# A two-block transformer kernel on one core: the first weight slab of each stage in two pieces, two slabs' low halves on VectorE, token transposes at an earlier place

## The reference, cut to what matters

```python
# first block, twice (l = 0, 1)
h = rmsnorm(x, pre_g[l])
u_a, v_a, g_a, q, k, v, g_b = split(h @ w_in[l])            # 1024 -> 2816
y_a = u_a * (spatial_w @ layernorm(v_a) + spatial_b) * silu(g_a)
y_b = attention(rope(rmsnorm(q)), rope(rmsnorm(k)), v) * silu(g_b)
x = x + rmsnorm(concat(y_a, y_b) @ w_out[l], post_g[l])
# second block, once
h = concat(pad, meta_tokens, x)
sb_q, sb_k, sb_v, sw_q, sw_k, sw_v, sb_z, sw_z, g_sb, g_sw = split(rms_norm(h) @ w_in_2)
o_sb = stick_breaking_attention(sb_q, sb_k, sb_v)
o_sw = sliding_window_sink_attention(rope(sw_q), rope(sw_k), sw_v, sinks)
y = sigmoid(g_sb) * ((o_sb * silu(sb_z)) @ w_branch_sb) + sigmoid(g_sw) * ((o_sw * silu(sw_z)) @ w_branch_swa)
out = rms_norm(h + y @ w_out_2)[:, 128:]
```

## Time and profile before

| | us |
|---|---|
| median of 3 runs | 1041.55 (1040.52 to 1042.21) |
| the profiled execution | 1039.15 |
| its span, first to last instruction | 1037.4 |
| TensorE busy | 992.3 (96%) |
| VectorE busy | 631.5 (61%) |
| ScalarE busy | 478.0 (46%) |
| GpSimd busy | 249.3 (24%) |

### The profile page before, as it was taken

One profiled execution on the slowest core, in us unless ns is written; L12 is line 12 of the kernel. 1 busy time (PEld: TensorE's weight loads), 2 busy tenths in 40 slices (PEclk: granted clock), 3 DMA queues, 4 the chain that ended last, 5 costly groups with the idle time before them and its releaser, 6 DMA issues.

```text
span 1037.4 us, 13824 instructions
## 1 busy us (share of the span) xinstructions
PE 992.3 (96%) x5063; PEld 833.5 (80%) x5063; DVE 631.5 (61%) x937; ACT 478.0 (46%) x841; POOL 249.3 (24%) x168
## 2 busy tenths in 40 slices
PE   5999999999999999999999999999999889999996
PEld 4988888787888888787888989887788768888885
DVE  4677678827777688737346675598368883212203
ACT  4445665535435555435366666423556652222211
POOL 2216100002216000012331021135223433224251
PEclk9999999999999999999999999999999999999999
DMA  7332101232423001342221021122210103323312
...
DMA packets 66454, 80.44 MB, mean 78 GB/s; under 512 B 5440, under 2 KB 50624, under 8 KB 66384
## 3 DMA queue, kind: packets, MB, share of 16 engines
...
...
## 4 chain that ended last, share of the span: by engine, by line
PE 53%; issue 26%; DVE 12%; ACT 5%; POOL 2%; DMA 1%; POOLq 0%; SPq 0%; DVEq 0%; ACTq 0%
PE ps L1683 15%; PE ps L1684 14%; PE ps L1685 14%; DVE tokw L1530 2%; ACT pw L999 2%; PE ps L1725 1%; PE ps L1727 1%; PE ps L1726 1%; PE ps L1996 1%; DVE rot L1527 1%; ACT whi L823 1%; DVE wlo L1072 1%; DVE small L1605 1%; DMA raw<-in_w_in 1%; PE ps L2002 1%
## 5 line engine op out<-in xcount | busy, mean ns | idle before, releaser
L551 POOL TENSOR_TENSOR wlo<-raw,whi 128x2048 fp32r<-128x2048 f32 (+1 forms) x30 | 132.0, 4400 | 298.3 <-ACT whi L823 298.3
L1683 PE MATMUL ps<-whi,hhi 128*128 128x512 f32 (+1 forms) x320 | 116.7, 365 | 5.3 <-DVE hlo L1063 4.5
L1683 PE MATMUL ps<-hhi,whi 128*128 128x512 f32 x288 | 113.1, 393 | 3.1 <-DVE gate_sw L1565 2.4
L1685 PE MATMUL ps<-whi,hlo 128*128 128x512 f32 (+1 forms) x320 | 115.1, 360 | 0.0
L1684 PE MATMUL ps<-wlo,hhi 128*128 128x512 f32 (+1 forms) x320 | 115.0, 359 | 0.0
L1684 PE MATMUL ps<-hlo,whi 128*128 128x512 f32 x288 | 112.3, 390 | 0.0
L1685 PE MATMUL ps<-hhi,wlo 128*128 128x512 f32 x288 | 112.2, 390 | 0.0
L823 ACT ACTIVATE whi<-raw 128x2048 fp32r<-128x2048 f32 (+1 forms) x35 | 63.5, 1816 | 97.1 <-PE ps L1685 97.1
L1072 DVE TENSOR_TENSOR wlo<-raw,whi 128x2048 fp32r<-128x2048 f32 (+1 forms) x34 | 75.0, 2206 | 40.2 <-ACT whi L601 39.6
L601 ACT ACTIVATE whi<-raw 128x2048 fp32r<-128x2048 f32 (+1 forms) x34 | 61.7, 1815 | 78.3 <-PE ps L1685 75.6
L1725 PE MATMUL ps<-hhi,whi 128*128 128x512 f32 x192 | 78.2, 408 | 0.0
...
## 6 DMA issues: line engine op xcount, KB each, us to landing
...
```

What stands on the lines that cost most here:

```text
L551: pool.tensor_tensor(wlo[s][:, 0:n, :], raw[s][:, 0:n, :], whi[s][:, 0:n, :].bitcast(F32), ALU.subtract).then_inc(slab_split, 1)
L1683: pe.matmul(out_ap, lhsT=lhi(k), rhs=rhi(k), start=first and k == 0, stop=False, skip_group_check=True)
L1685: m = pe.matmul(out_ap, lhsT=llo(k), rhs=rhi(k), start=False, stop=last and k == n - 1, skip_group_check=True)
```

## The change

- **Start.** The first tile of x comes as two halves on two queues (SyncE's and ScalarE's), ScalarE's ahead of the norm gains and of tile 1. The loads of tiles 2 and 3 are issued later. TensorE turns the identity 16 times before the first tile.
- **First slab of each stage.** It is loaded, rounded and subtracted in two pieces of 1024 elements (`first_slab_hi`, `first_slab_low`), and unit (0, 0) waits for the pieces separately. VectorE makes the low halves of the tiles between the pieces.
- **Tiles 0 and 1** are both turned ahead of the last unit of the stage before.
- **End of a layer.** VectorE scales tile 2 (`post_scale`) before the first slab but adds it (`post_add`) only after the slab and three of four low halves of tiles 0 and 1. ScalarE sums output tile 3 ahead of tile 2's input sum, and both after the second slab's high half.
- **Second block.** The low halves of slabs 13 and 14 move from GpSimd to VectorE: 13 behind the rotation of tile 3's first half, 14 behind all rotations.
- **Transposes of tokens.** Pairs stand behind units 1 to 5, on all three engines.

```diff
@@ order of the first tiles
-TILE_AT = {0: 1, 3: 2, 4: 3}
+TILE_AT = {3: 2, 4: 3}
@@ sync: start
-            sp.dma_start(x[:, 0, :], a["x"][0, 0:P, :]).then_inc(x_loaded[0], 16)
+            sp.dma_start(x[:, 0, 0:512], a["x"][0, 0:P, 0:512]).then_inc(x_loaded[0], 16)
@@ sync: slab()
-                    sp.dma_start(wide(raw[i % RING]) if whole else raw[i % RING][:, :, 0:w], src)\
-                      .then_inc(w_loaded[i % RING], 16)
+                    if i == 0:
+                        for piece, loaded in enumerate((first_loaded, w_loaded[0])):
+                            at_ = bass.AP(src.tensor, src.offset + 2 * piece * P * DIN1,
+                                          [[DIN1, P], [P * DIN1, 2], [1, 512]])
+                            sp.dma_start(wide(raw[0])[:, 2 * piece:2 * piece + 2, :], at_).then_inc(loaded, 16)
+                    else:
+                        sp.dma_start(wide(raw[i % RING]) if whole else raw[i % RING][:, :, 0:w], src)\
+                          .then_inc(w_loaded[i % RING], 16)
@@ sync: slab2()
-                sp.dma_start(dst, src).then_inc(w_loaded[j % RING], 16)
+                if j == 0:
+                    sp.dma_start(dst[:, 0:2, :], src[:, 0:2, :]).then_inc(first_loaded, 16)
+                    sp.dma_start(dst[:, 2:4, :], src[:, 2:4, :]).then_inc(w_loaded[0], 16)
+                else:
+                    sp.dma_start(dst, src).then_inc(w_loaded[j % RING], 16)
@@ gpsimd: low halves of the second block
+                if j in (13, 14):
+                    continue
+                if j == 15:
+                    pool.wait_ge(slab_split, DEPTH * SLABS + RING + 15)
@@ scalar: start
+            act.dma_start(x[:, 0, 512:], a["x"][0, 0:P, 512:]).then_inc(x_loaded[0], 16)
...
+            def first_slab_hi(l, i, piece):
+                if piece == 0:
+                    act.wait_ge(first_loaded, l * 16 + 16 * (i // SLABS) + 16)
+                    act.wait_ge(unit_done, l * UNITS + UNITS_BY_SLAB[SLABS - RING] + UNITS * (i // SLABS - 1) + CREDIT)
+                else:
+                    act.wait_ge(w_loaded[0], l * (8 * SLABS) + 16 * (i // RING) + 16)
+                k = slice(4 * piece, 4 * piece + 4)
+                act.activation(whi[0][:, k, :], raw[0][:, k, :], ACT.Copy).then_inc(whi_done if piece else first_hi, 1)
...
-            act.wait_ge(x_loaded[0], 16)
+            act.wait_ge(x_loaded[0], 32)
             sum_x(0, 0, 0)
-            load_x(2)
             act.wait_ge(x_loaded[1], 16)
             sum_x(0, 0, 1)
+            load_x(2)
+            first_slab_hi(0, 0, 0)
             load_x(3)
-            act.dma_start(rope[:], a["rope1"].rearrange("c (t p) d -> p c t d", p=P)).then_inc(rope_loaded, 16)
-            split_hi(0, 0)
             transposed_x(0, 0, 0)
+            first_slab_hi(0, 0, 1)
+            act.dma_start(rope[:], a["rope1"].rearrange("c (t p) d -> p c t d", p=P)).then_inc(rope_loaded, 16)
@@ scalar: end of a layer
-                split_hi(l, SLABS)
+                first_slab_hi(l, SLABS, 0)
+                first_slab_hi(l, SLABS, 1)
                 transposed_x(l, 1, 0)
-                sum_next(2)
-                sum_out(1, 3)
                 transposed_x(l, 1, 1)
                 split_hi(l, SLABS + 1)
+                sum_out(1, 3)
+                sum_next(2)
@@ scalar: second block, loop over c
-                if 3 <= c < 7:
-                    tokens_transposed_hi(2 * c - 6)
-                    tokens_transposed_hi(2 * c - 5)
-            tokens_transposed_hi(8)
-            tokens_transposed_hi(9)
+                if 1 <= c < 6:
+                    tokens_transposed_hi(2 * c - 2)
+                    tokens_transposed_hi(2 * c - 1)
@@ vector: new function, start
+            def first_slab_low(l, i, piece):
+                if piece == 0:
+                    dve.wait_ge(first_hi, l + i // SLABS + 1)
+                else:
+                    dve.wait_ge(whi_done, l * SLABS + i + 1)
+                    dve.wait_ge(slab_split, l * SLABS + RING + i)
+                k = slice(4 * piece, 4 * piece + 4)
+                dve.tensor_tensor(wlo[0][:, k, :], raw[0][:, k, :], whi[0][:, k, :].bitcast(F32),
+                                  ALU.subtract).then_inc(slab_split if piece else first_low, 1)
+            def transposed_x(l, ahead, t, halves=(0, 1)):
+                for half in halves:
...
-            slab_low(0, 0)
-            transposed_x(0, 0, 0)
+            first_slab_low(0, 0, 0)
+            transposed_x(0, 0, 0, (0,))
+            first_slab_low(0, 0, 1)
+            transposed_x(0, 0, 0, (1,))
@@ vector: end of a layer (post_norm is split into post_scale and post_add)
-                post_norm(2)
-                slab_low(l, SLABS)
-                transposed_x(l, 1, 0)
-                transposed_x(l, 1, 1)
-                normalise(l, 1, 2)
+                post_scale(2)
+                first_slab_low(l, SLABS, 0)
+                transposed_x(l, 1, 0, (0,))
+                first_slab_low(l, SLABS, 1)
+                transposed_x(l, 1, 0, (1,))
+                transposed_x(l, 1, 1, (0,))
+                post_add(2)
                 slab_low(l, SLABS + 1)
-                post_norm(3)
+                transposed_x(l, 1, 1, (1,))
+                normalise(l, 1, 2)
+                post_scale(3)
+                post_add(3)
@@ vector: second block
+            def slab2_low(j):
+                dve.wait_ge(whi_done, DEPTH * SLABS + j + 1)
+                dve.wait_ge(slab_split, DEPTH * SLABS + RING + j)
+                low(wlo[j % RING][:], raw[j % RING][:], whi[j % RING][:]).then_inc(slab_split, 1)
...
+                    if (half, t) == (0, 3):
+                        slab2_low(13)
@@
+            slab2_low(14)
...
-                if 3 <= c < 7:
-                    tokens_transposed_lo(2 * c - 6)
-                    tokens_transposed_lo(2 * c - 5)
-            tokens_transposed_lo(8)
-            tokens_transposed_lo(9)
+                if 1 <= c < 6:
+                    tokens_transposed_lo(2 * c - 2)
+                    tokens_transposed_lo(2 * c - 1)
@@ tensor: start
+            for n in range(16):
+                pe.matmul(ps[:, F_BANK, 0:P], lhsT=ident[:], rhs=ident[:], is_transpose=True)
             x_transposed(0, 0, 0)
+            x_transposed(0, 0, 1)
@@ tensor: by_token_half (tokens_half of the second block is changed alike)
-                    product(ps[:, t, :], lambda k: hhi[:, 4 * half + k, t * P:t * P + P],
-                            lambda k: hlo[:, 4 * half + k, t * P:t * P + P], lambda k: hi[:, k, :], lambda k: lo[:, k, :],
-                            4, first=half == 0, last=half == 1).then_inc(unit_done, 1)
+                    m = None
+                    for at_ in (0, 2):
+                        if (i, t) == (0, 0):
+                            pe.wait_ge(*((slab_split, l * SLABS + RING + 1) if at_ else (first_low, l + 1)))
+                        m = product(ps[:, t, :], lambda k: hhi[:, 4 * half + at_ + k, t * P:t * P + P],
+                                    lambda k: hlo[:, 4 * half + at_ + k, t * P:t * P + P], lambda k: hi[:, at_ + k, :],
+                                    lambda k: lo[:, at_ + k, :], 2, first=half == 0 and at_ == 0,
+                                    last=half == 1 and at_ == 2)
+                    m.then_inc(unit_done, 1)
@@ tensor: first units; last unit of a layer
-                    if t == 0:
+                    if (i, t) == (1, 0):
...
+                        x_transposed(l, 1, 1)
@@ tensor: second block, loop over c
-                if 3 <= c < 7:
-                    tokens_transposed(2 * c - 6)
-                    tokens_transposed(2 * c - 5)
-            tokens_transposed(8)
-            tokens_transposed(9)
+                if 1 <= c < 6:
+                    tokens_transposed(2 * c - 2)
+                    tokens_transposed(2 * c - 1)
```

28 lines of the change are left out of this document (17 added, 11 removed).

## The result

The changed kernel's median is 1033.76 us (1032.94 to 1034.14, 4 executions), the kernel before's in the same session 1041.03 (1039.46 to 1042.21, 4 executions); the ratio is 0.9926, with a 95% interval of 0.9912 to 0.9939. It is faster by 0.7%.

What follows compares the result with a forecast made beforehand. The prediction took TensorE, busy for 992.3 of 1037.4 us, as the bound. Start -1.25, boundaries -0.2, second block -2.5 and -0.8 make -4.75 us, from 1041.55 to 1036.8, range 1033.8 to 1039.6.

Steps and rivals of the forecast that it cites:

- Start: At the kernel's start: first product 0.45 us sooner plus 0.8 from the half-clock stretch, -1.25 us in all.
- tile 1's landing: At the start: tile 1's transfer lands some 1.3 us later, at 9.7, with 0.25 MB added ahead on ScalarE's queue.
- The slow stretch: At the start: half of the 1.6 us lost at half clock comes back, 0.8 us gained.
- Boundaries: At the two layer boundaries: TensorE's wait moves to tile 3 rather than going, -0.1 us each, -0.2 for both.
- no wait at the first unit: Sign at each stage's first unit: TensorE doesn't wait there, but about 1.5 us for tile 3's `xs` at both boundaries.
- Second block: Second block: the waits ahead of unit 2 (-2.5 us) and for `tg` (-0.8 us) go.
- Its split: Second block: moving slabs 13 and 14 off GpSimd gives -2.5 us, the tokens' reordered transposes -0.8 us.
- The basis: Whole kernel: the runs' median stands 2.4 us above the profiled 1039.15, so the gain is taken off 1041.55.
- full boundaries: Rival at the boundaries: GpSimd's roots aren't held, tile 3 comes 0.8 us sooner at each, 1035.4 us; chance 0.13.
- A start that pays nothing: Rival at the start: tile 1 lands later than 9.7 or the half-clock stretch stays as long, 1038.0 us; chance 0.17.
- the rotations got short: Second block, against a rival: the 4.98 us rotation rows aren't GpSimd's doing and stay long, 1041.4 us; chance 0.05.
- no wait for issue: Boundaries, against a rival: TensorE pays ScalarE's 4.32 us issue wait at the split unit of both, 1045.4 us; chance 0.04.

Runs made afterwards that it cites:

- the twelve added transposes: Changed kernel with 8 more identity transposes between tile 0's and tile 1's transposes and 4 more ahead of the first product: 1032.2 us, ratio 0.9912.
- the run with the output root first: Changed kernel with GpSimd making tile 3's output root before tile 2's input root, and VectorE's order altered to match: 1033.78 us, ratio 0.9926.

## Why the prediction was wrong where it was

**Start (-1.25 predicted, -1.91 measured).** The failed step is tile 1's landing: "so it lands some 1.3 us later, at 9.7". It was summed from 8.55, 0.17 later than before. I had counted the bytes ahead of it on ScalarE's queue. But the half tile that was put there had stood on SyncE's queue, and the core's DMA engines were already full in the kernel before (window 4.5 to 8.4, DMA share 0.97):

```profile
4.50:8.40 3.90, 0.00 (x0) 0.00 (x0) 0.03 (x1) 1.17 (x3) 0.74 (x2) 1.00 0.97 363
```

The tile and the gains are the same bytes, and until tile 1's sum all queues together had moved about 2.15 MB before and 2.2 MB after.
The Trainium skill ("DMA: Bandwidth & Descriptors", "Queues, rings and completion order") says that SyncE's and ScalarE's queues each have a ring on the same 16 engines and no engine of their own; the landing 0.17 later instead of 1.3 agrees.
Everything behind it was right: from the sum's start to the end of `xs` 3.43 us (3.4 predicted), and 13.86 is 15.1 less 1.15 and a little. The slow stretch gave back less than the 0.8 I took: 1.91 - 1.69 (15.55 - 13.86) = 0.22.

This 0.22 is one pair of executions. The first product is steady: at 15.55 to 15.68 in five profiles with the old start, at 13.61 to 13.99 in five with the changed one. What the slow stretch costs behind it isn't. From the first product to the first milestone it took 181.5 us in the four profiles without such a stretch (one with the old start, three with the twelve added transposes), 182.84 to 183.31 in the other four with the old start, and 182.08, 182.84, 183.05, 184.35 and 184.35 with the changed one. So the term of the stretch was no gain that one could count on: all that is shown is the earlier product, 1.6 to 2.1 us.

Of TensorE's clock: a stretch at full speed with TensorE idle for 1.77 and 0.72 us came ahead of the half-clock one in the changed kernel; with transposes alone in part of them (1.30 and 0.29 us of idle time left), nothing fell.
By the rule of the Trainium skill ("TensorE: Matmul & The Clock Gate", Part 4) that transposes don't count as busy, those twelve should have changed nothing; the run with them is 1.6 us faster, and the measurement decides against the rule here.

**Boundaries (-0.2 predicted, +0.03 measured).** The mechanism held: the wait at the first unit went or shrank, `xs` of tile 3 was late in its place (1.48 at the second, 0.36 at the first), both GpSimd roots were held where I had put them. Wrong was "no wait at the first unit" for the first boundary, which waited 0.84 (0.58 in the second profile, nothing in that of the run with start and boundaries alone). The size can't be read from one pair: from the first milestone to the second the five profiles with the old boundaries take 294.32 to 295.29 us, the eight with the changed ones 294.17 to 294.91, with medians 0.27 apart.

**Second block (-3.3 predicted, -3.57 measured).** Right in every row: no `tokw` row over 1 us between 695 and 720, no wait ahead of unit 2, 1.30 for `kw`, none for `tg`. Its split was wrong: the transposes alone, which I had at 0.8, give 1.96 in their trace, and the slabs alone, at 2.5, give 2.63.
The Trainium skill ("SBUF — State Buffer", "Who interferes with whom") says that a VectorE instruction with two SBUF inputs contends with a GpSimd one that reads SBUF; the step of 2.25 us that takes 0.16 once GpSimd's low half is elsewhere bears it out, also for an operation of four columns.

**The basis (the step that cost most).** "The median of the runs stands 2.4 above that execution; on its basis the time is 1041.55 - 4.75". I carried these 2.4 us over as if they were the same in both kernels. They aren't: the profiled execution of the kernel before lay 1.88 us below its session's median (1041.03), that of the changed kernel 0.38 above its own. These 2.26 us are most of the 3.04 between 1036.8 and 1033.76; 0.52 is the median of three runs, 1041.55, that the session put at 1041.03; 0.26 is the sum (5.01 between the two profiled executions, not 4.75).

Where the missing time lies, the second profiles show in part. The kernel before has, in its second, 1.64 us of half-clock stretch behind unit 2's wait, and 0.90 more ahead of the second block, which no run places. Four profiles have a wait of 1.7 to 2.4 us at that point (the kernel before twice, start and boundaries alone, transposes alone), and two of them have the stretch. The ten without the wait have no half-clock stretch between 700 and 740. So the change takes that stretch away together with the wait, in the executions that had it. That the usual execution has it is likely (half of four profiles) but not shown.

Against it stands the stretch at 819, in both profiles of the changed kernel and in neither of the kernel before, though the wait ahead of it (1.8 us) is in all four. It is the 0.78 lost in the window stage: the run with the output root first has the same code there but no such stretch in its profile, and takes 240.71 us from the merge to the last projection, as the kernel before does, against 241.49.

That the sum came so near the profiles' difference was luck in part: start and second block gave 0.66 and 0.27 more than I had said, the boundaries 0.23 less, and the 0.78 wasn't in it.

What stays open: what decides whether a wait of about 2 us is followed by such a stretch. The same wait had it in some executions and not in others, at the start (1.8 us, none in the profile of the second block's part alone), ahead of unit 2 and in the window stage. How often, the runs don't say, since only the profiled executions show where a stretch lies.

The rivals: full boundaries failed by their mechanism, since the roots were held. A start that pays nothing failed by its first half, tile 1 wasn't late; its second, a slow stretch that costs as much as before, came true in most of the five profiles. As for the others, the rotations got short; no wait for issue came at the split units (TensorE's longest anywhere is 0.6 us).
